# Attention in one Trainium2 kernel: exponentials left undivided, outputs multiplied by transposed inverse totals

## The reference, cut to the part that the change touches

The reference is two transformer blocks on 512 tokens of width 1024. The change is in the attention of the first block: eight heads of dense causal attention ("mla") and eight of dilated attention ("dil"), whose three patterns the kernel adds up under one softmax.

## Time and profile before

| | us |
|---|---|
| median of 3 runs | 1746.5 (1745.69 to 1747.34) |
| the profiled execution, its own time | 1748.67 |
| its span | 1746.9 |
| PE busy over the span | 1690.5 (97%) |
| DVE, ACT, POOL busy over the span | 1095.9, 745.0, 299.9 |

### The profile page before, as it was taken

One profiled execution on the slowest core, in us unless ns is written; L12 is line 12 of the kernel. 1 busy time (PEld: TensorE's weight loads), 2 busy tenths in 40 slices (PEclk: granted clock), 3 DMA queues, 4 the chain that ended last, 5 costly groups with the idle time before them and its releaser, 6 DMA issues.

```text
span 1746.9 us, 32394 instructions
## 1 busy us (share of the span) xinstructions
PE 1690.5 (97%) x12765; PEld 1499.6 (86%) x12765; DVE 1095.9 (63%) x1756; ACT 745.0 (43%) x1111; POOL 299.9 (17%) x289
## 2 busy tenths in 40 slices
PE   5999999999999999899999999999999999999998
PEld 4776666788888888799999989999999999989986
DVE  6766586777774668855868664344753766754633
ACT  4467575454332342532322544346323643322323
POOL 2112296210000002432005221110102000000002
PEclk8999999999999999999999999999999999999999
DMA  9453532443333232264335752332543233332332
GB/s 316 118 141 100 157 111 87 130 99 104 99 95 97 85 108 69 87 168 128 124 106 162 218 138 86 98 118 79 165 116 97 73 94 91 92 97 85 96 95 75
DMA packets 321167, 201.18 MB, mean 115 GB/s; under 512 B 51279, under 2 KB 303814, under 8 KB 320918
## 3 DMA queue, kind: packets, MB, share of 16 engines
q1 hardware_dynamic: 300976, 160.79, 32.4%
q0 software_dynamic: 7952, 24.83, 4.7%
q10 hardware_dynamic: 12118, 13.88, 2.3%
HBM read 177.75 MB, written 17.24 MB: 112 GB/s over the span
## 4 chain that ended last, share of the span: by engine, by line
PE 84%; DVE 6%; ACT 4%; SPq 2%; issue 2%; DMA 1%; POOL 1%; ACTq 0%; DVEq 0%; POOLq 0%
PE ps L1476 69%; SPq L862 2%; PE ps L1617 1%; DVE wlo L2193 1%; PE ps L1778 1%; PE ps L1676 1%; PE ps L1788 1%; PE ps L1804 1%; PE ps L1691 1%; PE ps L1593 1%; PE ps L2036 1%; ACT whi L920 1%; PE ps L2130 1%; DMA xrow<-in_x_dram 1%; PE ps L1955 0%
## 5 line engine op out<-in xcount | busy, mean ns | idle before, releaser
L1476 PE MATMUL ps<-zhi,whi 128*128 128x258 f32 (+2 forms) x2072 | 639.4, 309 | 1.9 <-ACT ub L1209 0.7
L1476 PE MATMUL ps<-zlo,whi 128*128 128x258 f32 (+2 forms) x2072 | 633.8, 306 | 0.0
L1476 PE MATMUL ps<-zhi,wlo 128*128 128x258 f32 (+2 forms) x2072 | 632.4, 305 | 0.0
L1476 PEld LDWEIGHTS ps<-zhi,whi 128*128 128x128 f32 x2072 | 391.3, 189 | 26.0 <-issue 2.8
L2193 DVE TENSOR_TENSOR wlo<-stage,whi 128x1024 fp32r<-128x1024 f32 x256 | 325.6, 1273 | 133.8 <-ACT whi L920 121.9
L1476 PEld LDWEIGHTS ps<-zlo,whi 128*128 128x128 f32 x2072 | 390.5, 188 | 19.6 <-issue 1.2
L1476 PEld LDWEIGHTS ps<-zhi,wlo 128*128 128x128 f32 x2072 | 391.2, 189 | 18.1
L920 ACT ACTIVATE whi<-stage 128x1024 fp32r<-128x1024 f32 x256 | 269.5, 1055 | 303.5 <-PE ps L1476 253.8
L1476 PE MATMUL ps<-ghi,whi 128*128 128x512 f32 x340 | 134.7, 396 | 0.0
L1476 PE MATMUL ps<-glo,whi 128*128 128x512 f32 x340 | 134.3, 395 | 0.0
L1476 PE MATMUL ps<-ghi,wlo 128*128 128x512 f32 x340 | 134.0, 394 | 0.0
(11 more groups left out here) (441 smaller groups left out, 2815.4 us busy)
## 6 DMA issues: line engine op xcount, KB each, us to landing
stage<-in_w_up_dram SPq DMA_DIRECT2D x88, 512.0 KB, 3.8
stage<-in_w_in_dram SPq DMA_DIRECT2D x74, 512.0 KB, 3.9
stage<-in_w_down_dram SPq DMA_DIRECT2D x32, 512.0 KB, 4.0
ring<-in_w_ada_dram POOLq DMA_DIRECT2D x24, 512.0 KB, 4.4
adab<-in_w_ada_dram SPq DMA_DIRECT2D x16, 512.0 KB, 7.7
stage<-in_w_down_dram SPq DMA_DIRECT2D x16, 384.0 KB, 3.4
stage<-in_w_o_dram SPq DMA_DIRECT2D x8, 512.0 KB, 4.1
ring<-in_w_ada_dram SPq DMA_DIRECT2D x8, 512.0 KB, 3.8
```

The source lines that it names most:

```text
L1476: last = pe.matmul(out, w(a, k), x(k, t0, t1), start=(k == 0 and a is whi and x is x_hi), stop=(k == ks - 1 and a is wlo))
```

```diff
@@ ACT
             for t in range(NS + 5):
+                if t >= 7 and t % QB == 3:
+                    m = (t - 7) // QB
+                    act.wait_ge(inv_mm, m + 1)
+                    act.activation(rowinv[:, :], ps[:, 7 - m % 2, :], ACT.Copy).then_inc(inv_done, 1)
                 if t < NS:
                     exps(t, 0)
...
-                if t >= 7 and t % QB == 3:
-                    m = (t - 7) // QB
-                    act.wait_ge(at_o, QB * m + QB)
-                    act.activation(mhi[:, (m + 4) % 8, :], ps[:, 6 + m % 2, :], ACT.Copy).then_inc(mixhi, 1)
+                if t >= 8 and t % QB == 0:
+                    m = (t - 8) // QB
+                    act.wait_ge(mix_done, INV0 + m + 1)
+                    act.activation(mhi[:, (m + 4) % 8, :], mix[:, m % 2, :], ACT.Copy).then_inc(mixhi, 1)
@@ PE
-                    pe.wait_ge(at_p, 2 * q + r + 1)
+                    pe.wait_ge(at_exp, 2 * q + r + 1)
...
-                if i == 0 and m >= 2:
-                    pe.wait_ge(mixlo, m - 1)
+                if i == 0 and m:
+                    pe.wait_ge(inv_done, INV0 + m)
...
+            def inverse_rows(m):
+                pe.wait_ge(inv_wide, WIDE0 + m + 1)
+                if m:
+                    pe.wait_ge(mix_done, INV0 + m)
+                for i in range(QB):
+                    mm = pe.transpose(ps[:, 7 - m % 2, i * P:(i + 1) * P], invwide[:, i, :], const("ident"))
+                mm.then_inc(inv_mm, 1)
...
                 if 3 <= t < NS + 3:
                     turn(t - 3)
+                if t >= 6 and t % QB == 2:
+                    inverse_rows((t - 6) // QB)
@@ DVE
-                    dve.wait_ge(mixhi, m + 1)
-                    dve.tensor_tensor(mlo[:, (m + 4) % 8, :], ps[:, 6 + m % 2, :], mhi[:, (m + 4) % 8, :].bitcast(F32), ALU.subtract)\
-                       .then_inc(mixlo, 1)
+                    dve.wait_ge(at_o, QB * m + QB)
+                    dve.wait_ge(inv_done, INV0 + m + 1)
+                    if m >= 2:
+                        dve.wait_ge(mixlo, m - 1)
+                    dve.tensor_tensor(mix[:, m % 2, :], ps[:, 6 + m % 2, :], rowinv[:, :], ALU.mult).then_inc(mix_done, 1)
+            dve.wait_ge(mixlo, HEADS - 1)
+            dve.wait_ge(mixhi, HEADS)
+            dve.tensor_tensor(mlo[:, 3, :], mix[:, 1, :], mhi[:, 3, :].bitcast(F32), ALU.subtract).then_inc(mixlo, 1)
+            dve.wait_ge(mixlo, HEADS)
@@ POOL
-            for t in range(NS):
-                w = (STEPS[t][2] + 1) * P
-                pool.wait_ge(at_rec, t + 1)
-                for r in range(2):
-                    pool.tensor_scalar(pb[:, t % 4, r, 0:w], pb[:, t % 4, r, 0:w], total(t, r, 32), None, ALU.mult)\
-                        .then_inc(at_p, 1)
+            for m in range(HEADS):
+                pool.wait_ge(at_rec, QB * m + QB)
+                if m:
+                    pool.wait_ge(inv_mm, m)
+                pool.tensor_copy(invwide[:, :, :].rearrange("p i (r d) -> p (i r) d", r=2),
+                                 inverses(QB * m, QB).unsqueeze(2).to_broadcast([P, 2 * QB, HD])).then_inc(inv_wide, 1)
+                if m:
+                    k = (m + 3) % 8
+                    pool.wait_ge(mixhi, m)
+                    pool.tensor_tensor(mlo[:, k, :], mix[:, (m - 1) % 2, :], mhi[:, k, :].bitcast(F32), ALU.subtract)\
+                        .then_inc(mixlo, 1)
```

More of the change, by code:

```diff
@@ L289, in emit @@
         rtp = at("rtp", [P, 2, T1], TAB + 8192 + 4096)
+        mix = at("mix", [P, 2, T1], TAB + 8192 + 4096)
+        rowinv, invwide = at("rowinv", [P, T1], ZUO + 8192), at("invwide", [P, QB, P], ZUO + 10240)
         ring = [[at(f"ring{n}{i}", [P, D], b + 4096 * i) for i in range(RING)] for n, b in enumerate((FREE + 16384, ZUO))]
@@ L431, in emit @@
         at_pt = [sem("at_pt0"), sem("at_pt1")]
-        at_rec, at_p = sem("at_rec"), sem("at_p")
+        at_rec, inv_mm = sem("at_rec"), sem("inv_mm")
+        inv_done, mix_done, INV0 = xt_done, xt_mm, KD
+        inv_wide, WIDE0 = tab_ready, 2
         mixhi, mixlo = sem("mixhi"), sem("mixlo")
@@ L616, in least, with total, inverses @@
             return small[:, 8 + 2 * (t % 4) + r:9 + 2 * (t % 4) + r]
-        def total(t, r, base=16):
-            c = base + 2 * (t % 4) + r
+        def total(t, r):
+            c = 16 + 2 * (t % 4) + r
             return small[:, c:c + 1]
+        def inverses(t, n=1):
+            c = 32 + 2 * (t % 8)
+            return small[:, c:c + 2 * n]
         FFNS = [dict(T=T1, up="w_up", down="w_down", cw="cw", cb="cb", key="b1", g2=40),
@@ L2493, in _ @@
                     dve.wait_ge(at_exp, 2 * q + 2)
[L2494 to L2497, removed]
+                    if q >= 2 * QB:
+                        dve.wait_ge(inv_wide, WIDE0 + q // QB - 1)
+                    dve.reciprocal(inverses(q), small[:, 16 + 2 * (q % 4):18 + 2 * (q % 4)]).then_inc(at_rec, 1)
                 if 3 <= t < NS + 3:
```

## The result

Over 18 runs each, the changed kernel took 1751.36 us at the median (1748.51 to 1754.69) and the kernel before 1747.44 (1745.59 to 1749.91). The ratio is 1.0022, with an interval of 1.0016 to 1.0029, so it is 3.9 us slower. The forecast was 2.4 slower (1748.9, range 1746.5 to 1751.7): the time lies in the range near its upper end, and the interval lies on both sides of the 0.2% that the prediction took as the least it could tell from no change. Of the 2.5 us between 1748.9 and 1751.36, 0.9 is the median of the kernel before, 1746.5 over 3 runs and 1747.44 over 18. The direction was right; some 1.5 us were missing from the sum.

What follows compares the result with a forecast made beforehand. PE was taken to bound the mla half, with PE waiting mainly for ACT in the dil half. Terms -0.05 + 1.30 + 0.15 + 0.26 + 0.72 gave 2.4 us slower: 1746.5 + 2.4 = 1748.9 us, range 1746.5 to 1751.7.

Steps and rivals of the forecast that it cites:

- POOL's savings: Attention: removing POOL's multiplications gains PE 0.66 us in pair 0, with scores(7) 0.23 early, and nothing in the mla half.
- The dil half gives nothing: Pairs 0 to 2: shorter ACT runs and POOL's gain are eaten by the transposes, leaving 0.05 us gained in all.
- the slip of exps(9, 0): Dil half, pair 1: ACT's mhi copy waits for mix, so exps(9, 0), PT(6) and values(6) slip by some 0.25 us.
- The transposes: PE, four more per pair: 0.108 us each, 0.43 a pair; 1.30 slower over pairs 3 to 5, mla period 10.45.
- Steps 30 and 34: Pairs 6 and 7: transposes partly fill PE's waits of 0.28 and 0.17 us, leaving costs of 0.15 and 0.26.
- Rival A: Turn to inverse_rows boundary: added work costs more than its spacing, 1750.5 us, or 1752.8 if every idle spot refuses; chance 0.20.
- rowinv on ACT in the idle time: ACT, ahead of exps(4m+7, 0): the 0.48 us copy fits idle time of 0.60 (step 7) and 1.24 (step 27), no cost.
- POOL's new work: Attention: a copy and a subtraction per pair, 1.60 us each, hidden from PE; POOL's busy time falls to about 25 us.
- Rival C: Pair 0: POOL's first copy comes some 6 us late and holds PE 1.9 us in step 6: 1750.8 us; chance 0.03.
- The end: PE's last wait: mix, mhi, mlo in series, one operation of 0.69 us with its semaphore more: 0.72 slower.
- T2: Experiments' theory on the 1.56 us: it comes from something else the change does there, or the clock falls in any execution.
- T1: Experiments' theory on the 1.56 us: the clock falls because PE stands still 2.25 us; filling or shortening the wait removes it.

Runs made afterwards that it cites:

- e4_double: The changed kernel with each set of four transposes of invwide done twice, into the same bank; 1755.62 us, ratio 1.0044 to the kernel before.
- e1_fill: The changed kernel with 18 unused transposes on PE in its last wait, ahead of the last wo_first; 1750.68 us, ratio 1.0016 to the kernel before.
- e7a_after_hifirst: The changed kernel with the last wo_first doing its two mhi products first and waiting for mlo only ahead of the third; 1750.31 us, ratio 1.0017.
- e8a_after_both: The changed kernel with mhi products first in the last wo_first and ACT's split_hi of wo one step earlier; 1750.9 us, ratio 1.0019.
- e6_slow_end: The kernel before with two unread copies on ACT ahead of the last mhi, lengthening PE's last wait; 1749.82 us, ratio 1.0011.
- e2_noinv: The changed kernel without the rowinv and invwide copies and the transposes, mix multiplying by ones; 1748.71 us, ratio 1.001 to the kernel before.
- e3_late: The changed kernel with the rowinv copy as ACT's last operation of its step instead of the first; 1761.08 us, ratio 1.0087 to the kernel before.
- e9_after_again: The changed kernel once more, unchanged, for a second profile; 1751.02 us, ratio 1.0017 to the kernel before.

## Why the prediction came out as it did

**POOL's savings: right.** Pair 0 loses its wait for POOL; scores(7) start 10.97 us after the first scores (223.18 less 212.21) instead of 11.20, the 0.23 of the sum.

**The dil half gives nothing: right.** The two waits for ACT fell by 0.44 and 0.46, against 0.48 priced. From the first scores to the first mla turn it takes 32.89 us, before 32.91: 0.02 gained against 0.05. What the eased waits gave back (0.66 in pair 0, 0.44 and 0.46), three sets of transposes took, and the 0.22 ahead of values(6), which is the slip of exps(9, 0) that the sum had at 0.25.

**The transposes: right, a little too dear.** Three mla pairs cost 1.17 against 1.30; the period of a pair is 10.39, where 10.45 was foretold. The price of 0.108 each was confirmed twice (0.44 for four in the chain; 0.43 in e4_double); what I left out is that small gaps of 0.04 to 0.06 ahead of the first values of a pair vanish behind them. Steps 30 and 34 together cost 0.16 instead of 0.41: from the turn at 276.26 to the last wo_first 23.67 us pass, before 22.66, and 0.85 of the 1.01 is the end. Rival A, a start of their own for each four, falls.

**rowinv on ACT in the idle time: right.** The timeline of ACT after:

```profile
274.06 0.58 ACT L1157 ACTIVATE rowinv<-ps 128x512 f32<-128x512 f32 x1
275.65 0.72 ACT L1150 ACTIVATE pb<-pb,small 128x512 f32<-128x512 f32 x1 [1.01 <-DVE small L2505]
```

The copy runs where ACT stood idle, and ACT still waits 1.01 us for DVE behind it; in step 7 it fills the 0.60 us of the earlier trace rows. exps(7, 0) starts 1.89 us after scores(7) there, before 1.90.

**POOL's new work: right that it is hidden, priced too high.** The groups of POOL in the attention:

```profile
L3106 POOL TENSOR_TENSOR mlo<-mix,mhi 128x512 fp32r<-128x512 f32 x7 | 8.9, 1272 | 12.5 <-ACT mhi L1174 12.5
...
L3101 POOL COPY invwide<-small 128x512 f32<-128x512 f32 x8 | 4.9, 612 | 57.5 <-DVE small L2520 57.5
```

A copy takes 0.61 us and a subtraction 1.27, where I took 1.60 for each; POOL is busy 13.8 us, not 25. PE never waits for it. The room that I gave the copy was misread: turn(7) ends at about 232.6, where the scores behind it start, not at 232.1, so it was 6.2 us and not 5.7, which changes nothing. Rival C, a first copy that is 6 us late, did not occur: it starts at 217.95 and takes 0.61.

**The end: the step that fell short.** I wrote "one 0.69 with its semaphore more: 0.72". The wait itself grew by 0.84 (1.41 to 2.25): mix takes 0.70, the copy to mhi 0.64 instead of 0.60, and there are more semaphores between. The missing term is what comes behind: PE stood still long enough for the clock to fall, and 27 matmuls took 1.56 us more. With that the term is 2.4 instead of 0.72, and the sum 2.4 - 0.72 + 2.4 = 4.1, against 3.72 measured between the marks; the transposes, priced 0.38 too high, are what is left. I priced a wait only by its own length, and none of my rivals had a clock in it. So the direction and the attention were foretold by their mechanism, but that the time still lies in the range is in part luck: the range ends where it does because of rival A, which did not occur, and it covers a loss of that size from a cause that I had not thought of. (Rival A's far price is 1748.9 + 3.8 = 1752.7, not 1752.8.)

That the fall goes with the wait is shown between the marks, in one profile of each kernel: three kernels without the long wait do not have it (e1_fill, e7a_after_hifirst and e8a_after_both), and the kernel before gets it with a longer wait (e6_slow_end). The length alone does not settle it. Open is why e2_noinv, at 2.24 us, kept its clock, as did e3_late behind its second wait of 2.20, and why elsewhere waits of 1.27 and 0.93 us were followed by a fall in some executions: one profile each doesn't tell a difference in what PE did before from chance. T2's second half holds for the rest of the kernel: there such stretches do come and go between executions.

That whole launches get the 1.56 us back is not shown. e1_fill and e7a_after_hifirst lie at 1.0016 and 1.0017 of the kernel before, and the unchanged code in e9_after_again at 1.0017. The mean granted clock of the launches is 0.9906 in the 29 of the changed kernel, 0.9921 in the 76 of the kernel before beside the experiments, 0.9928 in e1_fill and 0.9916 in e7a_after_hifirst. That points the way of T1, but e8a_after_both has 0.991 and e2_noinv 0.9913 without the fall in their profiles.

## What to carry to other kernels

Work that is taken from an engine that is busy but not waited for buys nothing, and work that is given to the engine that bounds costs its full spacing: here 58 us off POOL and 3.5 us onto PE made the kernel slower. Where PE must wait at the end of a stage, add up the whole serial chain of the other engines, and keep a term for the clock: here a wait of 2.25 us cost 1.56 us more in clock and one of 1.45 at the same place nothing, and in the profile it was enough to let PE start with the operand that is ready first. That makes 1.45 us no safe length: elsewhere in the same traces falls stand behind waits of 1.27 and 0.93 us. In a kernel whose runs scatter by several microseconds, put marks on the timeline of the bounding engine and compare the distances between them.

## What was unexpected of the hardware

The granted clock fell to 0.50 behind waits of 2.20 to 2.39 us in six cases of eight, in a kernel whose PE is busy 97%; at the end of the attention the fall cost about 1.5 us. 18 transposes whose result nobody reads, 2.19 us of PE, kept it at 1.00. And one kind of work on DVE got quicker when POOL had less work beside it: DVE's seven sums of 128x1024 with both inputs in SBUF took 1434 ns each before and 1323 after, while its 16 wide mask operations, which read PSUM, stayed at 686 and 685. The other kernels with POOL's multiplications have 1413 to 1436 ns for these sums, the others without them 1321 to 1341. The sums before, then groups of DVE after:

```profile
L2366 DVE SCALAR_TENSOR_TENSOR asum<-ring,csil,asum 128x1024 f32<-128x1024 f32 x7 | 10.0, 1434 | 0.0
```

```profile
L2505 DVE CUSTOM_DVE_ANT_0 pb<-ps,cst 128x512 f32<-128x512 f32 x16 | 10.4, 685 | 1.9 <-PE ps L1791 1.9
L2390 DVE SCALAR_TENSOR_TENSOR asum<-ring,csil,asum 128x1024 f32<-128x1024 f32 x7 | 9.3, 1323 | 0.0
```

It goes the other way too where POOL's new work meets DVE's: a `split_lo` (128x1024) on DVE at 230.48 took 1.96 us, with POOL's subtraction running from 230.10 for 1.27, and 1.22 in the kernel before; in e2_noinv it was POOL's subtraction at 228.15 that took 2.29 instead of 1.27, beside a `split_lo` at 228.09. Both operations take two inputs from SBUF. Why one or the other gives way is open.
